# The up blocks of a Strassen feed-forward computed product by product, two halves of the moving side in one matmul

## The chip, the cores and the metric

The kernel runs on one core of one Trainium2 chip. The metric is the device time of that core in microseconds (us), from one launch. [...]

## The reference, cut to what matters

One decoder layer for 512 positions and a model width of 2048, all in float32. The change lies in the last part, a gated convolutional MLP:

```python
h = rmsnorm(x, pre_ffn_g[l])
up = causal_depthwise_conv(h @ w_up[l], conv_w[l], conv_b[l])     # 2048 -> 2 x 5632, 3 taps
gate, val = jnp.split(up, 2, axis=-1)
y = (jax.nn.gelu(gate, approximate=True) * val) @ w_down[l]       # 5632 -> 2048
x = x + rmsnorm(y, post_ffn_g[l])
```

## The kernel before, in words

**Numbers.** Every float32 matrix is split into a rounded part `hi` (fp32r) and the rest `lo`. ACT makes `hi` by a copy with rounding, DVE makes `lo` by a subtraction. A product of two matrices is three passes on PE (`passes`, lines 922 to 924): hi x hi, hi x lo, lo x hi.

**Blocks.** The feed-forward goes through `w_up` in 22 blocks of 256 gate columns and 256 value columns. The first is computed plainly; the other 21 (called s = 1 to 21 here) by Strassen's method in Winograd's form: seven products P1, P2 and Q3 to Q7 of quarter matrices instead of eight. Each product runs over a contraction of 1024, which is 8 steps of 128 rows (`KH`), for two groups of 128 output columns. Between the up blocks stands the down projection of the group before, for s = 2 to 19 again as seven products, each of 12 matmuls of 512 columns (`down_quads`); s = 20 and 21 have a plain one (`down`). A block and the down products behind it are called a half; odd and even halves alternate.

**Order within an up block.** `up` runs `quad` for i = 0 to 7. A quad is one contraction step of all seven products: 7 products x 2 column groups x 3 passes of 256 columns, 42 matmuls, into seven PSUM banks that are all open through the block. So a block needs 336 matmuls of 256 columns.

**What feeds a quad.** SP brings one chunk of weights (128 x 1024, 512 KB) for each quad into the ring `w_raw` of four slots; chunk n + 4 waits until slot n has been read out (`lo_ready`). Three of the seven stationary tiles are quarters of the weights; four are sums, which DVE makes in three instructions (`quad_sum_one`, lines 2755, 2761, 2766: 512, 256 and 256 columns). ACT rounds 768 columns of raw weights (line 1813) and 1024 columns of sums (line 1818); DVE makes both `lo` parts (lines 2777 and 2783). The split weights `w_hl` hold two quads.

**After a block** ACT copies P1's bank (line 1832) and DVE puts the seven banks together into the four quarters of the output (`u_early`, `u_late`, `u_last`; lines 2868 to 2883), in the time of the down products. Those start with quarter weights (`raw_form_hi`, `raw_form_lo`) and go on to sums of quarters (`first_sum`, `second_sum`, `right_sum`, `third_sum`; lines 2833 to 2847, their `lo` parts line 2810). ACT carries each down product out of PSUM (`leave_product`, line 1911), and POOL adds it to a scratch in HBM by a DMA (line 824). In the same queue DVE does the convolution's taps (line 2900), gate x value (line 2921), and once for each pair of halves, within the even block, the sums and `lo` parts of the activations for the down products (lines 2934 to 2967).

**Order on the queues** is written by hand: `quad_round` and the dictionaries of tasks on DVE and ACT say behind which quad each of the other tasks stands. Every engine works its own queue strictly in that order.

**Elsewhere in the kernel** the input projections already run in the other way: `chain_half` (lines 1109 and 1111) takes one product at a time over half a contraction, with hi and lo of the moving side side by side in one matmul of 512 columns (hi x hi and hi x lo), and lo x hi in one of 256.

Of the kernel before, what the change touches and what calls it, by code (L numbers as in the profile page):

```python
# [24 lines left out]
F32 = mybir.dt.float32  # L25
# [63 lines left out]
RAW_PLACE = {P1: 0, Q3: 4, P2: 6}  # L89
COLUMN = {P1: 0, Q3: 1, P2: 2, Q5: 3, Q7: 4, Q6: 5, Q4: 6}  # L90
SPLIT_W = 7 * HB
RAW_W = 3 * HB
DOWN_BANKS = (7, P1, Q6, P2, Q7, Q4, Q3, Q5)
# [3 lines left out]
FORM_SLOT = (0, 1, 3, 2, 0, 3, 2)  # L97
# [3 lines left out]
AFTER_SUBS = (Q3, Q5, P1, Q6, P2, Q7, Q4)  # L101
# [13 lines left out]
def sums_before(g, e):  # L115
    w = half_index(g, e)
    return KH + PER_HALF * min(w, QUAD_HALVES) + KH * max(w - QUAD_HALVES, 0)
# [40 lines left out]
def build_layer(nc, xT, x, w, rope, decay, mix_g, ws_t, ln_g, ln_b, b_s, post_mix_g, pre_ffn_g, conv,  # L158
                post_ffn_g, rs_dram, x2_dram, y8_dram, gates_dram, sgu_dram, ret_dram, out):
    with ExitStack() as ctx:  # L160
# [13 lines left out]
        b_hi = at("b_hi", 64, [NG, S], F32R)  # L174
        b_lo = at("b_lo", 80, [NG, S], F32R)
# [20 lines left out]
        r3_hi = at("r3_hi", 160, [KH, HB], F32R)  # L196
        r3_lo = at("r3_lo", 168, [KH, HB], F32R)
        r4_lo_b = at("r4_lo_b", 188, [KH // 2, HB], F32R)
        r4_hi = at("r4_hi", 192, [KH, HB], F32R)
        r4_lo_a = at("r4_lo_a", 200, [KH // 2, HB], F32R)  # L200
# [116 lines left out]
        sums_even = flat[:, 0:4 * HB].rearrange("p (a s) -> p a s", a=2)  # L317
        sums_odd = wsum_odd
# [36 lines left out]
        def sums(i):  # L355
            return sums_odd if i % 2 else sums_even

        def product_form(k):
            a = FORM_SLOT[k] * 2 * CK * NB
            return w_flat[:, a:a + CK * NB], w_flat[:, a + CK * NB:a + 2 * CK * NB]  # L360

        def form_room(k):
            a = FORM_SLOT[k] * 2 * CK * NB + CK * NB
            return w_gap[:, :, :].rearrange("p a s -> p (a s)")[:, a:a + CK * NB]
# [34 lines left out]
        def operand(p, k):  # L399
# [9 lines left out]
            return hi.rearrange("p a s -> p (a s)"), lo.rearrange("p a s -> p (a s)")  # L409

# [47 lines left out]
        rs_row = ps[P1]  # L458

# [152 lines left out]
        out_done = sem("out_done")  # L612

# [304 lines left out]
        def _(pe):  # L918
# [321 lines left out]
            def quad(c, i, order, free={}):  # L1240

                pe.wait_ge(lo_ready, c + (i + 1))
                w_h, w_l = quad_split(i)
                for p in order:
                    if p in free:
                        pe.wait_ge(*free[p])
                    for n in range(2):
                        col = slice(COLUMN[p] * HB + n * P, COLUMN[p] * HB + n * P + P)
# [120 lines left out]
        def _(act):  # L1369
# [604 lines left out]
            def quads(c, n, tasks):  # L1974

                for i in range(2, KH):
                    quad_hi(c, i, c + (i - 1))
                    quad_sum_hi(n + i, i)
                    if i in tasks:
                        tasks[i]()  # L1980
# [1285 lines left out]
```

## Time and profile before

| | us |
|---|---|
| median of 3 runs | 2534.92 |
| lowest, highest | 2531.77, 2536.95 |
| the profiled execution | 2535.78 |
| its span, first to last instruction | 2533.9 |

The page of the profile gives busy time by engine (PE 2516.5 us, DVE 2075.3, ACT 1332.9) and the granted clock of PE. How long work takes is the duration in the rows; how fast an engine gets through a queue is the distance between starts, which is shorter, since an instruction starts before the one ahead of it has quite ended. An idle time in a row is followed by what ended it.

### The profile page before, as it was taken

The page shows a single profiled execution, that of the slowest core. Times are in us where ns is not written, and L with a number is a line of the kernel's source. Part 1 is how long each engine was busy: PE and PEld are TensorE (multiplying, and loading weights), DVE is VectorE, ACT ScalarE, POOL GpSimd, SP SyncE. Part 2 cuts the span into 40 slices and gives each one's busy share as a digit, 9 for nine tenths or more (in the row PEclk, how much of TensorE's full clock was granted, in tenths as well). Part 3 has the DMA queues.
Part 4 walks back from the last instruction along what each step waited for, and adds up shares of the span by engine and source line. Part 5 has one row for each costly group of instructions (what it writes and reads, how often), then busy time and mean ns, then how long its engine had stood idle before and what let it go on. Part 6 is the DMA issues. An engine that isn't in the chain of part 4 may idle for free. (4 is left out here: it accounts for less than half of the span.)

```text
span 2533.9 us, 40321 instructions
## 1 busy us (share of the span) xinstructions
PE 2516.5 (99%) x15762; PEld 2272.9 (90%) x15762; DVE 2075.3 (82%) x2517; ACT 1332.9 (53%) x1690; POOL 184.4 (7%) x271
## 2 busy tenths in 40 slices
PE   9999999999999999999999999999999999999998
PEld 8888888888888888888999999999999999999997
DVE  8898888888888545436898989898999989898987
ACT  8554545555555322335545656555555555555544
POOL 0100000000000000000000011100000000001122
PEclk9999999999999999999999999999999999999999
DMA  6434343333243723434234466666666666666878
GB/s 258 146 114 144 125 141 115 106 120 120 97 161 133 283 99 133 148 126 172 81 104 167 159 174 174 177 173 174 173 171 167 167 161 163 167 166 160 256 234 289
DMA packets 106765, 405.42 MB, mean 160 GB/s; under 512 B 12432, under 2 KB 12448, under 8 KB 100960
## 3 DMA queue, kind: packets, MB, share of 16 engines
q1 hardware_dynamic: 72576, 263.76, 30.7%
q0 software_dynamic: 33728, 138.71, 21.1%
q8 instruction: 124, 2.03, 0.3%
q10 hardware_dynamic: 288, 0.52, 0.1%
q14 instruction: 49, 0.40, 0.0%
HBM read 303.33 MB, written 95.42 MB: 157 GB/s over the span
## 5 line engine op out<-in xcount | busy, mean ns | idle before, releaser
L922 PE MATMUL ps<-h_both,w_hl 128*128 128x256 f32 (+1 forms) x1360 | 416.2, 306 | 1.0 <-DVE w_hl L2783 0.8
L923 PE MATMUL ps<-h_both,w_hl 128*128 128x256 f32 (+1 forms) x1360 | 415.4, 305 | 0.0
L924 PE MATMUL ps<-h_both,w_hl 128*128 128x256 f32 (+1 forms) x1360 | 415.4, 305 | 0.0
L1813 ACT ACTIVATE w_hl<-w_raw 128x768 fp32r<-128x768 f32 x168 | 142.3, 847 | 342.1 <-PE ps L924 342.1
L1109 PE MATMUL ps<-rm_both,w_hl 128*128 128x512 f32 x896 | 318.2, 399 | 1.3 <-DVE w_hl L2262 0.8
L922 PEld LDWEIGHTS ps<-h_both,w_hl 128*128 128x128 f32 x1360 | 259.8, 191 | 13.6 <-DVE w_hl L2783 1.5
L923 PEld LDWEIGHTS ps<-h_both,w_hl 128*128 128x128 f32 x1360 | 259.9, 191 | 11.2
L924 PEld LDWEIGHTS ps<-h_both,w_hl 128*128 128x128 f32 x1360 | 259.8, 191 | 11.2
L922 PE MATMUL ps<-w_hl,h_both 128*128 128x512 f32 (+1 forms) x684 | 261.6, 382 | 1.1 <-issue 0.6
L923 PE MATMUL ps<-w_hl,h_both 128*128 128x512 f32 (+1 forms) x684 | 261.2, 382 | 0.0
L924 PE MATMUL ps<-w_hl,h_both 128*128 128x512 f32 (+1 forms) x684 | 261.0, 382 | 0.0
L1111 PE MATMUL ps<-rm_both,w_hl 128*128 128x256 f32 x896 | 250.5, 280 | 0.0
L1109 PE MATMUL ps<-h_both,w_hl 128*128 128x512 f32 x672 | 237.8, 397 | 1.6 <-DVE shared L2323 1.3
L2125 DVE TENSOR_TENSOR w_hl<-w_raw,w_hl 128x1024 fp32r<-128x1024 f32 x75 | 91.4, 1223 | 161.7 <-ACT w_hl L1386 161.0
L2777 DVE TENSOR_TENSOR w_hl<-w_raw,w_hl 128x768 fp32r<-128x768 f32 x168 | 160.4, 955 | 61.0 <-ACT w_hl L1813 60.9
L1109 PEld LDWEIGHTS ps<-rm_both,w_hl 128*128 128x128 f32 x896 | 168.2, 188 | 42.4 <-DVE w_hl L2262 1.4
L1504 ACT ACTIVATE w_hl<-w_t 128x1024 fp32r<-128x1024 f32 x108 | 114.4, 1060 | 158.3 <-PE ps L1111 85.3
L922 PE MATMUL ps<-r_hi,w_hl 128*128 128x256 f32 x672 | 190.2, 283 | 0.6 <-ACT work L1911 0.6
L924 PE MATMUL ps<-r_hi,w_hl 128*128 128x256 f32 x672 | 190.2, 283 | 0.0
L923 PE MATMUL ps<-b_lo,w_hl 128*128 128x256 f32 x672 | 190.2, 283 | 0.0
L922 PE MATMUL ps<-b_hi,w_hl 128*128 128x256 f32 x672 | 190.2, 283 | 0.0
L924 PE MATMUL ps<-b_hi,w_hl 128*128 128x256 f32 x672 | 190.2, 283 | 0.0
(387 smaller groups left out, 6463.8 us busy)
## 6 DMA issues: line engine op xcount, KB each, us to landing
w_raw<-in_w SPq DMA_DIRECT2D x487, 512.0 KB, 3.8
y_scratch<-work POOLq DMA_DIRECT2D x78, 512.0 KB, 9.5
y_scratch<-forms_f POOLq DMA_DIRECT2D x29, 512.0 KB, 13.0
y_scratch<-big POOLq DMA_DIRECT2D x27, 512.0 KB, 7.6
gate_scratch<-mixing POOLq DMA_DIRECT2D x8, 1024.0 KB, 6.1
mixing<-in_x POOLq DMA_DIRECT2D x4, 1024.0 KB, 6.7
mixing<-mixing POOLq DMA_DIRECT2D x16, 256.0 KB, 3.7
merged<-gate_scratch POOLq DMA_DIRECT2D x4, 1024.0 KB, 12.6
```

What stands on the lines that cost most here:

```text
L922: pe.matmul(bank, s_hi, m_hi_, start=first, stop=False, skip_group_check=skip)
L923: pe.matmul(bank, s_hi, m_lo_, start=False, stop=False, skip_group_check=skip)
L924: return pe.matmul(bank, s_lo, m_hi_, start=False, stop=last, skip_group_check=skip)
L1109: pe.matmul(bank.rearrange("p (a s) -> p a s", a=2), s_h, m_both, start=p in (P1, Q5) and k == 0, stop=False, skip_group_check=True)
L1111: mm = pe.matmul(bank[:, 0:HB], s_l, m_h, start=False, stop=k == KH - 1, skip_group_check=True)
L1504: act.activation(w_hl[:, form_slot(n, f), 0, :], src, ACT.Copy, scale=-1.0 if p in (Q6, Q7) else 1.0)\
L1813: act.activation(hi[:, 0:RAW_W], w_raw[:, i % RING, HB:], ACT.Copy).then_inc(hi_ready, 1)
L2125: TTm(w_hl[:, j, 1, :], w_raw[:, j, :], w_hl[:, j, 0, :].bitcast(F32), ALU.subtract).then_inc(lo_ready, 1)
L2777: TTm(lo[:, 0:RAW_W], w_raw[:, i % RING, HB:], hi[:, 0:RAW_W].bitcast(F32), ALU.subtract)
```

## The change

All 21 up blocks now run as the input projections do. A block is 14 half-forms f = 0 to 13: product f // 2 of the chain P1, Q5, Q6, Q3, Q7, P2, Q4, half f % 2 of its contraction. A half-form is 4 steps x 2 column groups x (one matmul of 512 + one of 256), and takes one of four slots of `w_hl`, each 1024 columns wide:

```diff
-            def quad(c, i, order, free={}):
...
-                for p in order:
...
-                    for n in range(2):
-                        col = slice(COLUMN[p] * HB + n * P, COLUMN[p] * HB + n * P + P)
-                        mm = passes(ps[p][:, n * HB:n * HB + HB], (w_h[:, col], w_l[:, col]), operand(p, i),
-                                    i == 0 and n == 0, i == KH - 1, True)
...
+            def up_half_form(s, f):
+
+                p, a, slot = CHAIN[f // 2], f % 2, slots_of(s)[f % RING]
...
+                pe.wait_ge(*up_lo_made(s, f))
...
+                if p == Q6 and a == 0:
+                    pe.wait_ge(up_seeded, s)
+                if p == Q3 and a == 0:
+                    pe.wait_ge(u_step, 6 * s - 5)
+                if p == Q7 and a == 0:
+                    pe.wait_ge(u_step, 6 * s - 4)
+                if p == Q4 and a == 0:
+                    pe.wait_ge(u_step, 6 * s - 2)
+                for kk in range(4):
+                    k = 4 * a + kk
+                    o_h, o_l = operand(p, k)
+                    for m in range(2):
+                        bank, c = pair[:, m * NB:m * NB + NB], slice(kk * HB + m * P, kk * HB + m * P + P)
+                        pe.matmul(bank.rearrange("p (a s) -> p a s", a=2), w_hl[:, slot, 0, c], operand_both(p, k),
+                                  start=p in (P1, Q5) and k == 0, stop=False, skip_group_check=True)
+                        mm = pe.matmul(bank[:, 0:HB], w_hl[:, slot, 1, c], o_h, start=False, stop=k == KH - 1,
+                                       skip_group_check=True)
```

The products add up in three pairs of banks. `u_step` counts DVE's steps of a block in the order q5, x2, c12, c22, c11, c21: so f6 waits for q5 (`up_q5`), f8 for x2 (`up_x2`), f12 for c22. ACT copies one half of a pair out for each (`up_half_q5` and its like) and once seeds a pair from another (`up_seed`). The sums of weights are made for half a product at a time, in `up_t`, with t-one from chunks a and 2 + a, t-two adding chunk 4 + a, t-three and t-four:

```diff
+            def up_t_one(s, a):
...
+                TTm(up_t[a], up_raw(s, a), up_raw(s, 2 + a), ALU.add).then_inc(lo_ready, 1)
...
+            def ups(s, tasks, start=2):
+
+                for f in range(start, FORMS):
+                    if f == 7:
+                        up_q5(s)
+                    if f == 9:
+                        up_x2(s)
+                    if f == 12:
+                        up_c12_first(s)
+                    if f == 13:
+                        up_c22_first(s)
+                        up_c12(s)
+                        up_c22(s)
+                    up_lo_of(s, f)
...
+                    if f in (3, 4):
+                        up_t_two(s, f - 3)
...
+                    if f in tasks:
+                        tasks[f]()
...
             def quad_half(g, e, tasks):
...
+                third_sum(s)
+                up_lo_of(s + 1, 0)
+                sum_form_lo(s, 6)
+                up_t_one(s + 1, 0)
+                up_lo_of(s + 1, 1)
+                up_t_one(s + 1, 1)
                 if e:
                     gate_taps(g, e)
```

`up_lo_of` stands at line 2904 or 2906 of the changed kernel, t-one at 2920, t-two 2925, t-three 2931, t-four 2938, the steps c12 and c22 at 3006 to 3022, taps at 3045, down `lo` parts at 2942. On ACT the matching end of a half reads: down form 6, hi of f0, leave 4, hi of f1, leave 5, leave 6, then for odd halves `gate_linear`, and then hi of f2:

```diff
                 leave_product(g, e, 3)
-                sum_form_hi(g, e, 6)
-                quad_hi(c, PER_HALF, c + PER_HALF - 1)
-                quad_sum_hi(n + PER_HALF, PER_HALF)
+                sum_form_hi(s, 6)
+                up_hi(s + 1, 0)
                 leave_product(g, e, 4)
+                up_hi(s + 1, 1)
                 leave_product(g, e, 5)
...
                 leave_product(g, e, 6)
```

Line 824's stores, the number and size of chunks and the rule by which SP waits stay as they are; the order of the quarters in the chunks changes.

**DVE at the end of an odd half's down products.** Before, from `third_sum` (L2847): three small sums of quad 0, the `lo` of the last down form (L2810), the parts of quads 0 and 1; the taps follow behind four more rows of quads 1 and 2.

```order
L2847 TENSOR_TENSOR w_gap<-big,w_raw 128x1024
L2755 TENSOR_TENSOR big<-w_raw 128x512
L2761 TENSOR_TENSOR big<-big,w_raw 128x256
L2766 TENSOR_TENSOR big<-big,w_raw 128x256
L2810 TENSOR_TENSOR w_hl<-w_gap,w_hl 128x1024
L2777 TENSOR_TENSOR w_hl<-w_raw,w_hl 128x768
L2755 TENSOR_TENSOR w_gap<-w_raw 128x512
L2783 TENSOR_TENSOR w_hl<-big,w_hl 128x1024
L2761 TENSOR_TENSOR w_gap<-w_gap,w_raw 128x256
L2766 TENSOR_TENSOR w_gap<-w_gap,w_raw 128x256
L2755 TENSOR_TENSOR big<-w_raw 128x512
```

Now, from `third_sum` (L2982) at the same place:

```order
L2982 TENSOR_TENSOR w_gap<-big,w_raw 128x1024
L2906 TENSOR_TENSOR w_hl<-w_raw,w_hl 128x1024
L2942 TENSOR_TENSOR w_hl<-w_gap,w_hl 128x1024
L2920 TENSOR_TENSOR big<-w_raw 128x1024
L2906 TENSOR_TENSOR w_hl<-w_raw,w_hl 128x1024
L2920 TENSOR_TENSOR ps<-w_raw 128x1024
L3045 SCALAR_TENSOR_TENSOR big<-big,shared 128x511 x2
L3045 SCALAR_TENSOR_TENSOR big<-big,shared 128x510 x2
L2906 TENSOR_TENSOR w_hl<-big,w_hl 128x1024
```

The `lo` of f0 now stands ahead of the last down form's, and the sum of chunks 1 and 3 (L2920 into ps) and four taps stand ahead of the `lo` of f2.

**DVE at the end of an even up block.** Before, the last activation parts, then the down forms, with the recombination (L2868 to L2873) among them:

```order
L2959 TENSOR_TENSOR h_both<-big,h_both 128x2x256
L2965 TENSOR_TENSOR f_lo<-work,f_hi 128x1024
L2967 TENSOR_TENSOR s_lo<-big,s_hi 128x512
L2833 TENSOR_TENSOR big<-w_raw 128x1024
L2810 TENSOR_TENSOR w_hl<-w_raw,w_hl 128x1024 x2
L2868 TENSOR_TENSOR big<-ps,big 128x2x256
L2869 TENSOR_TENSOR big<-ps,big 128x2x256
```

Now, from t-four (L2938):

```order
L2938 TENSOR_TENSOR big<-big,w_raw 128x1024
L2938 TENSOR_TENSOR ps<-ps,w_raw 128x1024
L3104 TENSOR_TENSOR h_both<-big,h_both 128x2x256
L3006 TENSOR_TENSOR big<-ps,big 128x2x256
L2906 TENSOR_TENSOR w_hl<-big,w_hl 128x1024
L3110 TENSOR_TENSOR f_lo<-work,f_hi 128x1024
L3112 TENSOR_TENSOR s_lo<-big,s_hi 128x512
L3012 TENSOR_TENSOR big<-big,ps 128x2x256
L3017 TENSOR_TENSOR big<-ps,big 128x2x256
L3022 TENSOR_TENSOR big<-big,ps 128x2x256
L2906 TENSOR_TENSOR w_hl<-ps,w_hl 128x1024
```

L3022 is the step c22 for which PE's f12 waits; it now stands inside the block, behind the activation parts.

## Rows read from the trace of the kernel before

**Rows 1.** The page: the span, and busy time of each engine (share, instructions).
```profile
span 2533.9 us, 40321 instructions
PE 2516.5 (99%) x15762; PEld 2272.9 (90%) x15762; DVE 2075.3 (82%) x2517; ACT 1332.9 (53%) x1690; POOL 184.4 (7%) x271
```
**Rows 2.** Waits of PE over the whole span: us in total, times, longest.
```profile
PE ps L1109 <- DVE shared L2323: 1.3, 2, 0.8
...
PE ps L922 <- DVE w_hl L2783: 0.8, 2, 0.6
```
**Rows 3.** Busy time by stretch: input projections, then up blocks (us, engines, clock, DMA).
```profile
400.00:600.00 200.00, 199.30 (x1194) 175.46 (x1193) 167.20 (x195) 111.74 (x183) 8.28 (x14) 1.00 0.35 113
...
2000.00:2200.00 200.00, 200.00 (x1443) 190.04 (x1443) 182.45 (x242) 116.62 (x136) 18.76 (x22) 1.00 0.67 177
```
**Rows 4.** PE in order of time, an up block: start us, duration us, line.
```profile
1655.08 0.28 PE L923 MATMUL ps<-h_both,w_hl 128*128 128x256 f32 x1
...
1659.88 0.28 PE L924 MATMUL ps<-h_both,w_hl 128*128 128x256 f32 x1
```
**Rows 5.** PE in order of time, the last down products, and the next block's first matmul.
```profile
1696.12 0.39 PE L924 MATMUL ps<-w_hl,f_lo 128*128 128x512 f32 x1
...
1702.24 0.39 PE L924 MATMUL ps<-w_hl,h_both 128*128 128x512 f32 x1
1702.47 0.28 PE L922 MATMUL ps<-r_hi,w_hl 128*128 128x256 f32 x1
```
**Rows 6.** PE in order of time, an input projection with 512 and 256 columns alternating.
```profile
299.65 0.39 PE L1109 MATMUL ps<-h_both,w_hl 128*128 128x512 f32 x1
299.88 0.27 PE L1111 MATMUL ps<-h_both,w_hl 128*128 128x256 f32 x1
...
303.81 0.39 PE L1109 MATMUL ps<-h_both,w_hl 128*128 128x512 f32 x1
```
**Rows 7.** DVE in order of time, an up block and the recombination behind it.
```profile
1601.17 1.22 DVE L2783 TENSOR_TENSOR w_hl<-big,w_hl 128x1024 fp32r<-128x1024 f32 x1
1602.31 0.42 DVE L2766 TENSOR_TENSOR w_gap<-w_gap,w_raw 128x256 f32<-128x256 f32 x1
1602.65 1.40 DVE L2900 SCALAR_TENSOR_TENSOR big<-big,shared 128x510 f32<-128x510 f32 x2
1603.97 0.68 DVE L2755 TENSOR_TENSOR big<-w_raw 128x512 f32<-128x512 f32 x1
...
1622.91 0.68 DVE L2868 TENSOR_TENSOR big<-ps,big 128x512 f32<-128x512 f32 x1
1623.51 0.68 DVE L2869 TENSOR_TENSOR big<-ps,big 128x512 f32<-128x512 f32 x1
```
**Rows 8.** ACT in order of time: activation parts, P1's copy, a down form's hi.
```profile
1665.20 0.61 ACT L1944 ACTIVATE h_both<-work 128x512 fp32r<-128x512 f32 x1
1665.72 1.04 ACT L1945 ACTIVATE h_both<-big 128x1024 fp32r<-128x1024 f32 x1
...
1679.59 0.58 ACT L1832 ACTIVATE big<-ps 128x512 f32<-128x512 f32 x1
...
1690.59 1.06 ACT L1928 ACTIVATE w_hl<-w_gap 128x1024 fp32r<-128x1024 f32 x1 [3.16 <-DVE w_gap L2842]
```
**Rows 9.** DVE in order of time, the down products of one half into the next block.
```profile
1697.47 1.22 DVE L2810 TENSOR_TENSOR w_hl<-w_gap,w_hl 128x1024 fp32r<-128x1024 f32 x1
...
1703.82 0.69 DVE L2755 TENSOR_TENSOR big<-w_raw 128x512 f32<-128x512 f32 x1 [1.74 <-DMA w_raw<-in_w]
...
1707.62 0.69 DVE L2755 TENSOR_TENSOR w_gap<-w_raw 128x512 f32<-128x512 f32 x1 [0.43 <-DMA w_raw<-in_w]
```
**Rows 10.** Transfers of chunks 1 and 2, issued at 1693.1 and 1693.7: us from issue to landing.
```profile
DMA to landing us min/median/max: 4.4/7.3/10.1
```
**Rows 11.** The same of chunk 3, issued at 1698.8.
```profile
DMA to landing us min/median/max: 8.8/8.8/8.8
```
**Rows 12.** The page's DMA issues: KB each, median us from issue to landing.
```profile
w_raw<-in_w SPq DMA_DIRECT2D x487, 512.0 KB, 3.8
```

More of the change, by code:

```diff
@@ L1255, in up @@
-            def up(c, free, order=ORDER):
-                for i in range(KH):
-                    quad(c, i, *((order, free) if i == 0 else (ORDER,)))
+            def up_half_form(s, f):
+                p, a, slot = CHAIN[f // 2], f % 2, slots_of(s)[f % RING]
+                x, y, z = chain_banks(s)
+                pair = {Q5: z, Q3: z, P2: y}[p] if p in (Q5, Q3, P2) else x
+                pe.wait_ge(*up_lo_made(s, f))
+                if p == P1 and a == 0:
+                    if s == 1:
+                        pe.matmul(y[:, 0:NB], h_hi[:, 0, 0:P], h_hi[:, 0, :], start=True, stop=True)
+                        pe.wait_ge(plain_left, 2)
+                    elif s == 2:
+                        pe.wait_ge(u_step, 3)
+                    else:
+                        pe.wait_ge(*pair_left(s, "x"))
+                if p == Q5 and a == 0:
+                    if s == 1:
+                        pe.wait_ge(plain_left, 3)
+                    elif s == 2:
+                        pe.wait_ge(u_step, 6)
+                    else:
+                        pe.wait_ge(*pair_left(s, "z"))
+                if p == Q6 and a == 0:
[15 more added lines that the diff above has]
+                                       skip_group_check=True)
+                mm.then_inc(up_used(s, f)[0], 1)
@@ L1974, in quads @@
[L1974 to L1980, printed above, removed]
-            quads(C_SUB1, 0, {2: lambda: gate_linear(0, 0), 3: lambda: val_linear(0, 0), 4: lambda: gelus(0)})
-            quad_hi(C_LOOP, 0, C_LOOP - 1)
-            quad_sum_hi(KH, 0)
-            leave_p1(1)
-            quad_hi(C_LOOP, 1, C_LOOP)
-            quad_sum_hi(KH + 1, 1)
@@ L1989, in quad_half @@
[L1989 to L2001 removed]
+            up_hi(1, 0)
@@ new lines, in _, with ups @@
+            up_hi(1, 1)
+            act.wait_ge(r_lo, 4 * TT)
+            for t in range(4):
+                bank = done(A, FFN_USE, t, C_SUB1)
+                dst = (u_gate, u_val)[t // 2][:, t % 2, :]
+                act.activation(dst, bank, ACT.Copy).then_inc(plain_left, 1)
+            def ups(s, tasks):
+                for f in range(2, FORMS):
+                    if f == 5:
+                        up_seed(s)
+                    if f == 7:
+                        up_half_q5(s)
+                    if f == 9:
+                        up_half_x2(s)
+                    up_hi(s, f)
+                    if f in tasks:
+                        tasks[f]()
@@ L3215, in sub @@
     def sub(n):
-        quads(np.concatenate([a[:, n * HB:n * HB + HB] for a in (gate, val)], axis=1))
+        chain(np.concatenate([a[:, n * HB:n * HB + HB] for a in (gate, val)], axis=1))
     add(np.concatenate([gate[:, :HB], val[:, :HB]], axis=1))
```

682 lines of the change are left out of this document (371 added, 311 removed).

## The prediction

> **What bounds the kernel now.** The page comes first: PE is busy 2516.5 of 2533.9 us, DVE 2075.3, ACT 1332.9 [rows 1]. The list of PE's waits is short, and its longest entries for DVE come to 1.3 and 0.8 us over the whole run [rows 2]. So PE's own stream is the bound, and what shortens it shortens the kernel, as long as the others keep up. How much room they have is read by stretch: in the input projections, which already run in the new form, DVE is busy 167.20 of 200 us; in the up blocks it is 182.45 of 200 [rows 3]. That 9% is all the slack there is where the change lands, and PE's clock shows 1.00 in both.
>
> **What the stream gains.** In an up block the matmuls of 256 columns start 40 intervals apart in 4.80 us, 0.120 us each [rows 4]. In the down products 27 intervals of 512 columns take 6.12 us, 0.2267 us each [rows 5]. Where 512 and 256 alternate, twelve pairs take 4.16 us, 0.3467 us a pair [rows 6]: the sum of the two. A triple of 256 takes 0.360 us, so a pair saves 0.0133 us. That is one instruction's overhead; the columns are the same 768. A block has 7 x 8 x 2 = 112 triples: 112 x 0.0133 = 1.49 us, and 21 blocks give 31.4 us. A half (block and down products) is now 336 x 0.120 + 84 x 0.2267 = 40.32 + 19.04 = 59.36 us, and without any wait would be 38.83 + 19.04 = 57.87. A half-form takes 8 x 0.3467 = 2.77 us, a down product 12 x 0.2267 = 2.72.
>
> The Trainium skill (TensorE: Matmul & The Clock Gate, on back-to-back matmuls) puts the overhead of a warm matmul at about 2.5 ns above its columns. By it the saving would be 21 x 112 x 2.5 ns = 5.9 us, an estimate. The trace disagrees: 512 columns at 2.4 GHz are 213.3 ns and the starts are 226.7 apart [rows 5].
>
> **What DVE has to do.** Through a queue, 1024 columns cost DVE 1.14 us from start to start (1601.17 to 1602.31), a pair of taps 1.32, and 512 columns 0.60 (1622.91 to 1623.51) [rows 7]; whoever waits for one waits for its end, 1.22 or 0.68 after its start. For ACT the ends count: 1.04 to 1.06 us for 1024 columns, 0.61 for 512, 0.58 for a copy out of PSUM [rows 8]. A block's weight work on DVE is now 14 `lo` parts and 8 sums of 1024 and 8 steps of 512: 22 x 1.14 + 8 x 0.60 = 29.9 us, about what it was. So the amount is no term. The place is: six of the eight recombining steps move from the time of the down products into the block, where PE's f6, f8 and f12 wait for them, and the queue is in order.
>
> **The term that decides: chunk 3.** In the even halves DVE does the following between the sum of chunks 1 and 3 and the step c22: four taps 2.64, eleven `lo` (f2 to f12) 12.54, six sums 6.84, four more taps 2.64, gate x value 1.14, six steps 3.60, the activations' parts and sums 6.5. Together 35.9 us. PE goes from the start of f0 to the start of f12 in 12 x 2.77 = 33.3 us. So that sum must be done 2.6 us before f0 starts, or PE waits at f12 for all of the difference. It cannot be. Chunk 3 goes into the slot that the `lo` of the last down form sets free, and that `lo` ends 2.7 us before f0 at the earliest that matters, since PE's last down product (2.72 us) waits for it. (In the trace of before it ended at 1698.7 [rows 9], and chunk 3 was issued at 1698.8 [rows 11].) It may even end later: from the end of the fourth down product it takes `third_sum` 1.22, ACT's hi of the down form 1.05, ACT's hi of f0 0.95 more, then DVE's `lo` of f0 1.14 and the `lo` itself 1.22, with the hand-overs 5.9 us in all; PE has two products, 5.4 us, so it waits 0.45 us there in every half. Before, three small sums (1.3 us) stood there in place of the hi and `lo` of f0.
>
> How long chunk 3 takes to land I bound from both sides: chunk 1, alone in the queue, took 4.4 us, chunks 2 and 3, with stores around them, 10.1 and 8.8 [rows 10, 11]. In the trace of before they came 1.35 and 5.1 us after the block's start (1702.47 [rows 5] against 1703.82 and 1707.62 [rows 9]), and nobody on PE minded, since quad 2 is due only after 10 us. Now f2 is due 5.5 us after f0, and its `lo` stands behind the sum that needs chunk 3. I take 4.4 us behind the issue, the nearer row: DVE's queue in the down products is lighter by the recombination, so chunks 1 and 2 are asked for 11.8 us ahead of f0 (before: 1702.47 - 1693.1 = 9.4) and have landed when chunk 3 is asked for. Issued at f0 - 2.7, it lands at f0 + 1.7.
>
> **Even half, step by step**, in us after f0's start. Chunk 3 lands 1.7; sum 2.9; four taps to 5.5; `lo` of f2 ends 6.7, and f2 was due 5.55: PE waits **1.2**. Then `lo` f3, t-two, taps, `lo` f4, t-two, taps, `lo` f5 to 15.1, on time (f5 is due 15.1). Gate x value ends 16.2; ACT then rounds the activation's parts (0.52 + 0.95) and only then copies Q5's half, 18.3; q5 ends 19.0, f6 was due 17.8: **1.2**. `lo` f7, two sums t-three, two activation parts, `lo` f8, two activation sums, then x2, which ends 27.7; f8 was due 24.6: **3.2**. After that the hi of f11 waits for its slot, which PE leaves only at 30.5, and ACT's own activation parts; `lo` f11 starts 33.3; two t-four, an activation part, c12, `lo` f12, two activation parts, c22 first, c12, c22: 42.7. f12 was due 38.8: **3.9**. With 0.45 at the last down product the even half has 9.9 us of waits: 57.87 + 9.9 = 67.8 us.
>
> **Odd half.** No activation parts (6.5 us less), and the four early taps stand elsewhere. The same walk: f5 0.6 (t-two needs chunk 5, which is asked for only after chunk 3's sum), f6 1.9 (ACT has `gate_linear` ahead of Q5's copy), f8 1.0 (a tap pair ahead of x2), f12 0.6, the last down product 0.45: 4.5 us, 62.4 us.
>
> The same walk through the queues of before, with the same durations and the same rule for chunks, gives 59.4 us for a half, no wait of PE, and a wait of DVE for chunk 2 in each half, which is what the trace shows [rows 2, 9].
>
> **The sum.** Even blocks s = 4 to 18, eight: +79. Odd 5 to 19, eight: +36. s = 2 and 3, whose stores are lighter: +12. s = 1, 20, 21, with little beside them: +4. Less 31.4: +100 us. The profiled execution took 2535.8, so 2636; the median lies 0.9 below it: **2635 us**.
>
> **Ends of the range.** With every chunk landing 3.4 us after its issue (the page's median over all chunks is 3.8 [rows 12]) the walk still has 67.6 and 60.4 for the halves: about 2618. With 5 us behind each other, between the rows' 4.4 and 8.8, it has 69.6 and 65.5: about 2677. If my order of hand-overs is too strict everywhere except in the 35.9 us of the even half, what is left is 33.3 - 35.9, the chunk's landing at f0 + 0.7 and the sum: 5 us in nine even halves and 0.45 in eighteen, 53 - 31 = +22: 2557.
>
> **Rivals.** (1) Faster: the chain runs as it does in the input projections, where the longest entry among PE's waits is 1.3 us for all blocks together [rows 2]. Then the kernel gives 2535 - 31 = 2504. It decides at one point: the sum with chunk 3 must end 2.6 us ahead of f0. For it speaks that the total of DVE fits (92% of the time); against it, that there no down product stands between two blocks, and that DVE is at 84% [rows 3]. (2) DVE late only by the 35.9 us: 2557 to 2580. (3) The clock falls in the pauses of 3 to 4 us. The trace has only 1.00, and no PE wait above 2 us, so the price is bounded from the step: one half-form after each of the two long waits at 1.2 instead of 2.4 GHz costs 2 x 2.77 us in nine even halves, 50 us: 2685. The Trainium skill (TensorE: Matmul & The Clock Gate, on the clock gate) says that the clock falls to 1.2 GHz after an idle stretch; no row here shows one.
>
> **How the numbers follow.** Walk as forecast, 2590 to 2680: 0.80. Rival 1: 0.07. Rival 2: 0.06. Rival 3: 0.04. Something slight, within the bound: 0.03. The range 2570 to 2682 leaves out rival 1, the bottom of rival 2 and the clock's case. A measurement of this kernel can tell about 0.2% from no change, 5 us; faster by more 0.07, within 0.03, slower 0.90.
>
> **What would show it.** In the changed kernel's page, DVE and ACT lines as releasers of the 512-column matmul of the up blocks with some 110 to 130 us of idle in total, most of it under x2 and c22 in even halves; halves alternating near 68 and 62 us; a DVE wait for a transfer before the sum into ps; pairs 0.347 us apart in between. I am wrong if the list of PE's waits stays within a few us, or if the waits sit at `lo` parts alone, or if chunk 3 lands before f0.

## The result, and the profile after

The changed kernel takes 2698.57 us (median of 4 runs, 2698.15 to 2698.97); the kernel before took 2534.84 us in the same comparison (2531.77 to 2536.95). The ratio is 1.065, with a 95% interval of 1.0637 to 1.0664. The change costs 163.7 us. The prediction said 2635 with a range of 2570 to 2682: slower was right, the size was not, and the time lies outside the range.

The page of the changed kernel: span, busy time of each engine with its share and instructions, then the chain of work that ended last, by engine. In all rows PE is TensorE's matmuls, PEld its weight loads, DVE is VectorE, ACT ScalarE, POOL GpSimd, and SP is SyncE, whose queue issues the weight transfers.

```profile
span 2697.1 us, 35558 instructions
PE 2551.6 (95%) x13411; PEld 2173.1 (81%) x13411; DVE 2056.2 (76%) x2181; ACT 1386.8 (51%) x1732; POOL 184.9 (7%) x271
...
PE 58%; DVE 20%; DMA 9%; issue 6%; ACT 5%; SPq 0%; DVEq 0%; ACTq 0%
```

Against [rows 1], TensorE fell from 99% to 95% busy. Its busy time rose by 35 us all the same, though its stream is shorter: matmuls at a slower clock, which count as busy, are a part of it, and we come to them. Its waits (us in total, times, longest) stand against [rows 2]:

```profile
PE ps L1357 <- DVE w_hl L2906: 64.0, 18, 5.5
PE ps L1357 <- DVE big L3000: 29.7, 19, 2.8
PE ps L1357 <- DVE big L3022: 15.0, 10, 2.3
PE ps L1357 <- DVE big L2995: 12.1, 12, 4.2
PE ps L1005 <- DVE w_hl L2942: 6.6, 18, 0.4
```

L1357 is the new matmul of 512 columns. L3000 is x2, L3022 c22, L2995 q5, L2942 the `lo` of a down form: the four that the prediction names, with 63.4 us together. The largest entry is another one: 64.0 us behind a `lo` part, L2906. In order of time, one even half and the first wait of the odd half behind it (start us, duration, the wait in brackets; f0 starts at 1824.08 and 1896.48):

```profile
1834.88 0.79 PE L1357 MATMUL ps<-b_both,w_hl 128*128 128x512 f32 x1 [4.99 <-DVE w_hl L2906]
1848.82 0.47 PE L1357 MATMUL ps<-r_all,w_hl 128*128 128x512 f32 x1 [0.61 <-DVE big L2995]
1857.37 0.47 PE L1357 MATMUL ps<-r_both,w_hl 128*128 128x512 f32 x1 [2.76 <-DVE big L3000]
1871.05 0.47 PE L1357 MATMUL ps<-h_both,w_hl 128*128 128x512 f32 x1 [2.34 <-DVE big L3022]
...
1904.67 0.50 PE L1357 MATMUL ps<-b_both,w_hl 128*128 128x512 f32 x1 [2.38 <-DVE w_hl L2906]
...
```

The first row is f2, and it waits 4.99 us; the walk had given it 1.2. What VectorE did there, in order of time, against [rows 9]:

```profile
1819.96 1.22 DVE L2942 TENSOR_TENSOR w_hl<-w_gap,w_hl 128x1024 fp32r<-128x1024 f32 x1
1822.03 1.22 DVE L2920 TENSOR_TENSOR big<-w_raw 128x1024 f32<-128x1024 f32 x1 [0.86 <-DMA w_raw<-in_w]
1823.17 1.22 DVE L2906 TENSOR_TENSOR w_hl<-w_raw,w_hl 128x1024 fp32r<-128x1024 f32 x1
1829.82 1.23 DVE L2920 TENSOR_TENSOR ps<-w_raw 128x1024 f32<-128x1024 f32 x1 [5.42 <-DMA w_raw<-in_w]
1830.96 2.73 DVE L3045 SCALAR_TENSOR_TENSOR big<-big,shared 128x511 f32<-128x511 f32 x4
1833.60 1.22 DVE L2906 TENSOR_TENSOR w_hl<-big,w_hl 128x1024 fp32r<-128x1024 f32 x1
```

The `lo` of the last down form ends at 1821.2 and frees chunk 3's slot. Chunk 3 is asked for at 1821.3, which is f0 - 2.8, as the prediction had it. VectorE then stands still for 5.42 us. The transfer's own row (us from issue to landing), the answer to [rows 11]:

```profile
DMA to landing us min/median/max: 8.4/8.4/8.4
```

So chunk 3 lands at f0 + 5.7 and not at f0 + 1.7. Behind it come the sum, four taps and the `lo` of f2, and TensorE waits. The chain that ended last says the same, piece by piece (start us, us, what):

```profile
1821.34 8.36 DMA w_raw<-in_w
1829.82 1.23 DVE ps L2920
1831.05 2.65 DVE big L3045 x4
```

The clock did what the third rival said. Stretches of that half: us, busy time of PE, PEld, DVE, ACT and POOL, PE's granted clock, DMA share, GB/s.

```profile
1824.08:1829.90 5.82, 5.80 (x33) 4.78 (x31) 0.40 (x2) 3.38 (x4) 0.85 (x1) 1.00 1.05 261
1832.00:1834.80 2.80, 0.00 (x0) 0.00 (x0) 2.80 (x4) 1.02 (x2) 0.00 (x0) 0.50 1.07 234
1834.88:1837.00 2.12, 2.12 (x7) 1.83 (x8) 0.76 (x1) 1.33 (x2) 0.00 (x0) 0.50 0.65 245
1837.00:1840.00 3.00, 3.00 (x14) 2.57 (x14) 3.00 (x5) 1.37 (x2) 0.00 (x0) 0.70 0.00 0
1840.00:1848.00 8.00, 8.00 (x47) 6.85 (x45) 6.92 (x8) 5.72 (x9) 0.00 (x0) 1.00 0.00 1
```

In the last 2.8 us of the pause the granted clock is 0.50, that is 1.2 of 2.4 GHz, and f2 begins at that level. The last slow matmul of 512 columns starts at 1838.24 and takes 0.63 us, the next one 0.39; from 1840 on the row has 1.00. f2 to f5 take 13.3 us (from 1834.88 to 1848.82, less the 0.61 of f6's wait) in place of 4 x 2.77 = 11.1. Behind each of the eight waits at f2 of 4.8 us and more the work starts at 0.50. Behind the shorter ones of the odd halves it differs from half to half: it stays at 1.00 behind the 2.38 us at 1904.67, and is 0.50 in the 2.8 us behind waits of 2.45 and 2.44 us at 1630.6 and 1767.6. The Trainium skill (TensorE: Matmul & The Clock Gate, on the clock gate) says that the clock falls to 1.2 GHz after an idle stretch; the trace agrees for the wait of 5 us.

The last number in each row is worth a look too. While chunk 3 is on its way the DMA engines are busy all the time (1.05, 1.07: measured shares of 16 engines run slightly over 1); ten microseconds later they move nothing (0.00).

### The profile page after: what moved, and what is told of

It is laid out like the page before. It is cut to its first block, busy times and chain, and to the rows that moved or that the text cites. A ratio compares the mean times of both kernels' runs of the same rounds, so it can differ in the third digit from the quotient of the medians.

```text
span 2697.1 us, 35558 instructions
## 1 busy us (share of the span) xinstructions
PE 2551.6 (95%) x13411; PEld 2173.1 (81%) x13411; DVE 2056.2 (76%) x2181; ACT 1386.8 (51%) x1732; POOL 184.9 (7%) x271
## 3 DMA queue, kind: packets, MB, share of 16 engines
q0 software_dynamic: 33728, 138.71, 20.0%
## 4 chain that ended last, share of the span: by engine, by line
PE 58%; DVE 20%; DMA 9%; issue 6%; ACT 5%; SPq 0%; DVEq 0%; ACTq 0%
PE ps L1192 13%; PE ps L1005 8%; DMA w_raw<-in_w 8%; PE ps L1007 8%; PE ps L1006 8%; PE ps L1357 7%; PE ps L1194 7%; PE ps L1359 4%; DVE big L3045 3%; DVE w_hl L2904 2%; ACT w_hl L1925 2%; DVE w_hl L2906 2%; DVE w_raw L2931 1%; DVE w_hl L2942 1%; DVE w_hl L2407 1%
## 5 line engine op out<-in xcount | busy, mean ns | idle before, releaser
L1357 PE MATMUL ps<-h_both,w_hl 128*128 128x512 f32 x1008 | 358.3, 398 | 15.8 <-DVE big L3022 15.0
L1357 PE MATMUL ps<-b_both,w_hl 128*128 128x512 f32 x672 | 264.4, 431 | 66.1 <-DVE w_hl L2906 63.2
L1359 PE MATMUL ps<-h_both,w_hl 128*128 128x256 f32 x1008 | 282.9, 281 | 0.0
L1357 PEld LDWEIGHTS ps<-h_both,w_hl 128*128 128x128 f32 x1008 | 190.0, 188 | 64.2 <-issue 17.9
L1192 PE MATMUL ps<-h_both,w_hl 128*128 128x512 f32 x672 | 237.7, 397 | 1.3 <-DVE shared L2466 1.3
L1925 ACT ACTIVATE w_hl<-w_raw 128x1024 fp32r<-128x1024 f32 x168 | 176.5, 1051 | 97.0 <-DVE w_raw L2931 67.9
L1357 PEld LDWEIGHTS ps<-b_both,w_hl 128*128 128x128 f32 x672 | 139.1, 207 | 106.9 <-DVE w_hl L2906 68.6
L2268 DVE TENSOR_TENSOR w_hl<-w_raw,w_hl 128x1024 fp32r<-128x1024 f32 x75 | 91.4, 1223 | 162.5 <-ACT w_hl L1484 161.8
L1192 PEld LDWEIGHTS ps<-rm_both,w_hl 128*128 128x128 f32 x896 | 168.2, 188 | 42.4 <-issue 1.6
L1359 PE MATMUL ps<-b_both,w_hl 128*128 128x256 f32 x672 | 199.6, 297 | 0.0
L2906 DVE TENSOR_TENSOR w_hl<-w_raw,w_hl 128x1024 fp32r<-128x1024 f32 x126 | 153.8, 1221 | 58.4 <-ACT w_hl L1925 58.4
L1359 PEld LDWEIGHTS ps<-h_both,w_hl 128*128 128x128 f32 x1008 | 191.0, 189 | 0.8
L1194 PE MATMUL ps<-h_both,w_hl 128*128 128x256 f32 x672 | 187.8, 279 | 0.0
L1484 ACT ACTIVATE w_hl<-w_raw 128x1024 fp32r<-128x1024 f32 x71 | 74.8, 1057 | 204.1 <-PE ps L1007 202.0
L1194 PEld LDWEIGHTS ps<-rm_both,w_hl 128*128 128x128 f32 x896 | 169.1, 189 | 0.0
L1602 ACT ACTIVATE w_hl<-w_raw 128x1024 fp32r<-128x1024 f32 x108 | 114.0, 1056 | 95.4 <-PE ps L1194 92.2
```

Source lines behind the costliest of these rows:

```text
L1192: pe.matmul(bank.rearrange("p (a s) -> p a s", a=2), s_h, m_both, start=p in (P1, Q5) and k == 0, stop=False, skip_group_check=True)
L1194: mm = pe.matmul(bank[:, 0:HB], s_l, m_h, start=False, stop=k == KH - 1, skip_group_check=True)
L1357: pe.matmul(bank.rearrange("p (a s) -> p a s", a=2), w_hl[:, slot, 0, c], operand_both(p, k), start=p in (P1, Q5) and k == 0, stop=False, ...
L1359: mm = pe.matmul(bank[:, 0:HB], w_hl[:, slot, 1, c], o_h, start=False, stop=k == KH - 1, skip_group_check=True)
L1602: act.activation(w_hl[:, form_slot(n, f), 0, :], src, ACT.Copy, scale=-1.0 if p in (Q6, Q7) else 1.0)\
L1925: act.activation(w_hl[:, slots_of(s)[f % RING], 0, :], src, ACT.Copy, scale=-1.0 if p in (Q6, Q7) else 1.0)\
```

## The experiments

All of them start from the changed kernel unless said otherwise, and each was compared with the kernel before on the same chip, which took 2535.1 to 2535.7 us. To compare the kernels inside, the start of one operation is used, the first sum of the down forms, which occurs once in each half. In the changed kernel:

```profile
1734.86 1.21 DVE L2966 TENSOR_TENSOR big<-w_raw 128x1024 f32<-128x1024 f32 x1
...
1798.88 1.21 DVE L2966 TENSOR_TENSOR big<-w_raw 128x1024 f32<-128x1024 f32 x1
...
1871.96 1.21 DVE L2966 TENSOR_TENSOR big<-w_raw 128x1024 f32<-128x1024 f32 x1
```

One step is 64.0 us and the next 73.1. From the first to the eighteenth of these starts are 8.5 pairs of halves, and the table gives the mean pair. The two steps of a pair depend on where in its queue VectorE has this sum (the kernel before, with plain stores, shows 57.8 and 60.9, while TensorE has two equal halves), so the table compares only the pair.

| kernel | median us | pair of halves, us |
|---|---|---|
| before, plain stores | 2533.23 | 118.5 |
| changed kernel | 2698.57 | 136.1 |
| early release | 2637.12 | 129.1 |
| filled wait | 2702.76 | 136.3 |
| plain stores | 2634.84 | 128.8 |
| three passes | 2708.36 | 137.2 |
| early release, even halves reordered | 2594.35 | 124.2 |
| early release, short taps | 2602.28 | 126.0 |
| early release, plain stores | 2621.97 | 127.3 |
| both halves reordered | 2592.59 | 123.9 |
| even halves reordered, three passes | 2601.30 | 124.7 |
| both reordered, plain stores | 2562.13 | 120.7 |
| the same, three passes | 2564.26 | 120.7 |

### Chunk 3 is asked for earlier

Chunks 1, 2 and 3 of the next block may come when the last reader of their slots is done. These readers are `right_sum` and `third_sum`; the changed kernel waits for the `lo` parts behind them.

```
-                TTm(form_room(w, 4), down_raw(s, B22), down_raw(s, B12), ALU.subtract).then_inc(sum_ready, 3)
+                TTm(form_room(w, 4), down_raw(s, B22), down_raw(s, B12), ALU.subtract).then_inc(lo_ready, 2)
...
-                TTm(form_room(w, 6), down_sum, down_raw(s, B21), ALU.subtract).then_inc(sum_ready, 3)
+                TTm(form_room(w, 6), down_sum, down_raw(s, B21), ALU.subtract).then_inc(lo_ready, 1)
```

> The weight buffers of chunks 1 and 2 of the next block are handed back when the subtraction of the right sum has read them, and that of chunk 3 when the third sum has, no longer with the low parts of forms 4 and 6. Theory (chunk 3's landing sets f2): the transfer of chunk 3 starts some 3 us earlier, t-one of chunks 1 and 3 waits about 3 us less than the 5.3 us of the changed kernel, the wait at f2 falls from 5.0 us to about 2 in the even half, the clock stays at 1.00 there, and the pair of halves takes about 131 us in place of 137: 2640 to 2660 us. Rival (VectorE has too much to do anyway): the wait only moves from f2 to f6, f8 and f12, and the time is above 2685 us.

Measured: 2637.12 us (2632.97 to 2638.13), ratio 1.0403 (1.0386 to 1.0421), 61 us less than the changed kernel, and the clock over the run 0.995 in place of 0.981. TensorE's waits:

```profile
PE ps L1357 <- DVE big L3004: 30.3, 20, 2.8
PE ps L1357 <- DVE big L2999: 22.0, 18, 4.1
PE ps L1357 <- DVE big L3026: 16.2, 10, 2.4
PE ps L1357 <- ACT ps L1938: 9.7, 10, 1.1
...
PE ps L1357 <- DVE w_hl L2909: 4.2, 9, 0.9
```

The 64 us behind the `lo` of f2 (here L2909) are 4.2. The landing is as slow as it was (8.3 us); it only starts at 1793.7, 7.2 us ahead of f0 (1800.91), and so ends at f0 + 1.1. Some 18 us moved to q5 (L2999, 12.1 to 22.0) and to P1's copy (L1938, 1.5 to 9.7); the rest of the wait is gone, and with it 27 us of busy time (2551.6 to 2524.9), in which the slow matmuls behind the wait have their part. The first theory holds; the time lies 3 us below its range.

### The wait filled with matmuls

```
+                if f == 2 and s > 2:
+                    pe.wait_ge(*pair_left(s, "z"))
+                    for _ in range(20 if s % 2 == 0 else 8):
+                        pe.matmul(z[:, 0:NB].rearrange("p (a s) -> p a s", a=2), b_both[:, 0, 0, 0:P],
+                                  operand_both(Q5, 0), start=True, stop=True)
```

> While TensorE waits at f2 it now runs matmuls of 512 columns into the pair that Q5 is about to start: 20 in an even half (4.5 us at 0.2267), 8 in an odd one (1.8 us). They add nothing to the result. Theory (the pause costs clock): the granted clock stays at 1.00 through f2 to f5, which take 11.1 us in place of 13.05, and of that 2 us in each even half a part comes back at the end: 2660 to 2680 us. Rival (VectorE sets the pace, the slow matmuls ran in time that would have been waited): clock 1.00 too, but the waits at f6 and f8 grow by the same 2 us: 2693 to 2703 us. If the clock falls anyway, the pause is not its cause.

Measured: 2702.76 us (2697.83 to 2703.12), the pair 136.3. Two windows of an even half, the filled wait and the stretch behind it:

```profile
1832.43:1837.56 5.13, 4.73 (x23) 3.58 (x21) 5.00 (x6) 1.10 (x2) 0.00 (x0) 1.00 1.05 251
1837.56:1842.00 4.44, 4.44 (x25) 3.92 (x26) 3.08 (x4) 2.02 (x3) 0.00 (x0) 1.00 0.28 109
```

The clock stays at 1.00 here (over the whole run 0.994, against 0.981), so it was the pause that lowered it, and nothing is won: the waits at q5 and at f4, for P1's copy, grow from 12.1 and 1.5 us to 20.7 and 8.7 over the run. The rival holds. The slow matmuls ran in time that TensorE would have spent waiting for VectorE. The clock is a result of the wait and cost nothing here that could be measured.

### Plain stores, and the control

```
-                        pool.dma_start(y_range(e, p), staged_pair(stage(n)), accum_op=ALU.add).then_inc(landed, 16)
+                        pool.dma_start(y_range(e, p), staged_pair(stage(n))).then_inc(landed, 16)
```

> The stores of the down products write plainly in place of accumulating in memory, which leaves the accumulation over the groups out. Theory (the accumulating stores hold chunk 3 back): its landing falls from 8.4 us to about 5, the wait at f2 by about 3 us in each half, and the kernel takes 2640 to 2665 us. Rival (chunks 1, 2 and 3, asked for within 5 us, share the engines among themselves): the landing stays above 7.5 us and the time above 2690 us.

Measured: 2634.84 us (2629.21 to 2637.08), ratio 1.039 (1.0373 to 1.0407). Chunk 3 is asked for at 1801.6, which is f0 - 2.8 as in the changed kernel, and this is its landing:

```profile
DMA to landing us min/median/max: 3.7/3.7/3.7
```

That is one half. Over the sixteen halves s = 4 to 19 chunk 3 lands 3.5 to 6.6 us after its issue, 4.8 on average, against 8.2 to 9.1 and 8.5 in the changed kernel; the issue is at f0 - 2.7 or f0 - 2.8 in all of them. Chunk 4 is asked for 1.2 us behind it here, nearer than the 2.0 us of the changed kernel, so its neighbour among the chunks is not what made it slow. The time is 5 us below the theory's range.

The page's DMA queue of the stores (packets, MB, share of 16 engines) in this kernel:

```profile
q0 software_dynamic: 33728, 138.71, 14.4%
```

The changed kernel's page has, with the same bytes:

```profile
q0 software_dynamic: 33728, 138.71, 20.0%
```

So the accumulating stores take 1.4 times the engine time of plain ones for the same megabytes, and beside them the chunk lands after 8.5 us on average instead of 4.8. The control is the same edit in the kernel before:

> The control for the plain stores: the kernel before with stores that do not accumulate (the accumulation is left out). It has no wait for a chunk in these blocks, so the time should stay at 2535 us within 5. If it falls by more, a part of what plain stores gave the changed kernel had nothing to do with chunk 3.

Measured: 2533.23 us (2532.20 to 2534.78), ratio 0.9993 (0.9983 to 1.0002): no change. In this kernel the cost of the stores is paid only where somebody is waiting for a chunk.

### Both together

> Early release and plain stores together (the accumulation is left out). Each alone took the wait at f2 nearly away. If they remove the same wait, together they give little more than either: 2620 to 2637 us. If they act on different things (the one on when chunk 3 is asked for, the other on something that runs through the whole half), the gains add up: below 2600 us.

Measured: 2621.97 us (2619.36 to 2625.29). 15 us under early release alone, where the 61 and 64 us of each do not add up. In the main they remove the same wait, by its start and by its length; the number lies at the low end of what was expected.

### Three passes again

```
-                        pe.matmul(bank.rearrange("p (a s) -> p a s", a=2), w_hl[:, slot, 0, c], operand_both(p, k),
-                                  start=p in (P1, Q5) and k == 0, stop=False, skip_group_check=True)
+                        pe.matmul(bank[:, 0:HB], w_hl[:, slot, 0, c], o_h,
+                                  start=p in (P1, Q5) and k == 0, stop=False, skip_group_check=True)
+                        pe.matmul(bank[:, HB:], w_hl[:, slot, 0, c], o_l, start=False, stop=False, skip_group_check=True)
```

> The one matmul of 512 columns over hi and lo is taken apart again into two of 256; the order of the products and everything else stays. By the rows a block streams 1.49 us longer, 31.4 us in all. Theory (the waits hang on VectorE and the chunks, TensorE has slack beside them): most of it goes into shorter waits, some 0.2 us a half stay: 2700 to 2708 us. Rival (the chain goes through TensorE): the whole 31 us come on top, 2725 to 2732 us.

Measured: 2708.36 us (2707.83 to 2712.37), ratio 1.0682 (1.0664 to 1.07): 9.8 us above the changed kernel, just past the upper end of what the theory gave. The starts are the 0.120 us of [rows 4] again:

```profile
1850.59 0.28 PE L1357 MATMUL ps<-b_both,w_hl 128*128 128x256 f32 x1
1850.71 0.28 PE L1359 MATMUL ps<-b_both,w_hl 128*128 128x256 f32 x1
1850.83 0.28 PE L1360 MATMUL ps<-b_both,w_hl 128*128 128x256 f32 x1
```

In the changed kernel 21 pairs of one matmul of 512 and one of 256 columns, without a wait, lie between these starts:

```profile
1840.28 0.40 PE L1357 MATMUL ps<-b_both,w_hl 128*128 128x512 f32 x1
...
1847.70 0.40 PE L1357 MATMUL ps<-b_both,w_hl 128*128 128x512 f32 x1
```

That is 0.353 us a pair and not the 0.3467 of [rows 6]. The last up block (s = 21) has no wait in either kernel and takes 39.56 us merged, 40.31 us with three passes and in the kernel before: merging saves 0.75 us a block, 16 us in 21 blocks, half of the 31.4 that the expectation and the prediction count. 9.8 of the 16 reach the end. The kernel with three passes is the change without its merging: the new order alone costs 173 us (2708.4 - 2535.3). In the even half shown, the chain that ended last goes from chunk 3's landing to f12 through VectorE and ScalarE and not once through TensorE, so a shorter stream has nowhere to act there. In the odd half behind it the chain is back on TensorE from f8 on.

### VectorE's row in the even half

On top of the early release, the same operations in another order: x2 ahead of `lo` f8, the steps of c12 and c22 ahead of `lo` f12, the products behind q5, the first gate taps into the wait for chunk 3. ScalarE's row is reordered to match. From VectorE's row:

```
+                up_t_three(s, 0)
+                up_t_three(s, 1)
+                up_x2(s)
+                up_lo_of(s, 8)
+                first_forms_lo(g - 1)
...
+                up_t_four(s, 1)
+                up_c12_first(s)
+                up_c22_first(s)
+                up_c12(s)
+                up_c22(s)
+                up_lo_of(s, 12)
```

> On top of the early release, the even halves' work on VectorE and ScalarE stands in another order: the sums x2 and c12, c22 ahead of the low parts of f8 and f12, the products and first forms behind q5 and the low part of f6, the gate's first taps into the wait for chunk 3, its linear part ahead of the last product's leaving. No operation is added or left out. Theory (in the even half TensorE waits for the place of an operation in VectorE's row as much as for its amount): the waits at f4, f6 and f8 nearly go, f12 keeps some 3 us because VectorE has 56 us of work in a half of 58; an even half falls from 68.6 to 62 to 64 us, and the kernel takes 2570 to 2595 us. Rival (the amount alone decides, the waits only move): within 10 us of 2637.

Measured: 2594.35 us (2593.29 to 2599.36), ratio 1.024 (1.0222 to 1.0257). The order of the two rows was worth 43 us; the time is at the upper end of what was expected. The waits at f4, f6 and f8 of the even halves are gone, f12 keeps 1.6 us in most of them, and f5 has one of 0.4 to 1.1 us in some. The other side is the amount, tested by making the taps short:

```
-                    STT(buf[:, t, n:S], src[:, t, 0:S - n], col(t, k), buf[:, t, n:S], ALU.mult, ALU.add)\
+                    STT(buf[:, t, n:n + 1], src[:, t, 0:1], col(t, k), buf[:, t, n:n + 1], ALU.mult, ALU.add)\
```

> On top of the early release, each of the eight tap operations of a half of the feed-forward part works on one column instead of 510 or 511, so the convolution's taps are left out but for one column; every wait and signal stays. That takes some 4.9 us of VectorE's work from each half. Theory (VectorE is late in the even half, but in the odd half only the landings are): the even half falls by 3 to 5 us, the odd one by under 1 us, 2590 to 2612 us. Rival (not the amount of VectorE's work, but chains of single results): less than 10 us of gain in all.

Measured: 2602.28 us (2598.50 to 2603.20). The total is as expected, its places are not: both alternating distances fall by about the same (68.6 to 66.8 and 60.9 to 59.6). VectorE's busy time falls by 86 us (2055.5 to 1969.3), 3.9 for each of 22 blocks and not the 4.9 of the expectation, and some 8 us less work in a pair shorten it by 3.1. In the odd halves nearly every wait of TensorE is gone; in the even ones those at f6, f8 and f12 stay as they were (1.0, 2.7 and 0.6 to 2.4 us). Removing this work gave less than moving work did.

### The odd half, and what is left

```
+                    if f == 6 and s % 2:
+                        up_q5(s)
+                    if f == 8 and s % 2:
+                        up_x2(s)
```

> On top of the reordered even halves, the odd halves take q5 and x2 ahead of the gate's taps of f6 and f8. In the profile of the reordered kernel TensorE waits 1.16 us for q5 at f6 and 0.76 us for x2 at f8 in an odd half. Theory (these two wait for their place in VectorE's row): both go, some 1.5 to 1.9 us in each of ten odd halves: 2575 to 2582 us. Rival (what is gained at f6 and f8 is waited for at f10 to f12, since the taps then come later): 2590 to 2597 us.

Measured: 2592.59 us (2590.84 to 2595.27), no gain that can be told from none. The waits from f6 on in an odd half, first of the kernel with the even halves reordered, then of this one:

```profile
1869.83 0.47 PE L1357 MATMUL ps<-r_all,w_hl 128*128 128x512 f32 x1 [1.16 <-DVE big L3026]
1876.37 0.47 PE L1357 MATMUL ps<-r_both,w_hl 128*128 128x512 f32 x1 [0.76 <-DVE big L3031]
```

```profile
1874.83 0.47 PE L1357 MATMUL ps<-r_both,w_hl 128*128 128x512 f32 x1 [0.76 <-DVE big L3031]
1887.09 0.47 PE L1357 MATMUL ps<-h_both,w_hl 128*128 128x512 f32 x1 [0.71 <-DVE big L3053]
```

The first fence has q5 (L3026) and x2 (L3031). In the second, the wait for q5 is gone, the one for x2 is as long as it was, and there is a new one for c22 (L3053) at f12: the rival. What else is left shows in the chain that ended last of this kernel, ahead of another block:

```profile
1903.83 1.24 DVE w_gap L3013
1905.21 7.96 DMA w_raw<-in_w
1913.30 1.25 DVE ps L2951
1914.69 8.04 DMA w_raw<-in_w
1922.83 1.23 DVE ps L2956
```

Chunk 3's landing is followed by its sum, which frees a slot for chunk 5, whose landing is followed by the next sum (L2956). Two landings of 8 us stand behind each other between `third_sum` (L3013) and the `lo` of f5 (L2934), and the early release has only shortened what lies around them. That was tested with plain stores on this kernel, and both kernels with three passes beside it:

> The kernel with early release and both orders changed, with plain stores (the accumulation is left out). In the chain that ended last, that kernel's piece from 1842 to 1855 us is a store of 11.6 us whose landing ScalarE waits for before it writes the value tile; in its sister with three passes two landings of chunks, 8.6 and 8.5 us, stand in the same place. Theory (what is left behind TensorE's reordered row hangs on these landings): 2550 to 2575 us. Rival (VectorE's 107 us of work in a pair of halves of 124 set the rest): within 10 us of 2592.

> The kernel with early release and reordered even halves, and the one matmul of 512 columns taken apart into two of 256, as was done to the changed kernel itself, where it cost 9.8 us of the 31.4 that the rows give. TensorE now waits some 60 us in place of 130. Theory (the gain of the longer stream counts as far as the waits around it are gone): 15 to 28 us are lost here, 2609 to 2622 us. Rival (a fixed share of a third counts whatever the waits): 2602 to 2606 us.

> The same with the matmul of 512 columns taken apart into two of 256. Theory (with quick landings the chain runs through TensorE for more of the half, so the stream counts for more than the 7 to 10 us that it did until now): 15 us or more above the kernel with plain stores and one matmul. Rival (VectorE's chain in the even half absorbs it all the same): under 10 us above.

Measured: with plain stores 2562.13 us (2560.67 to 2562.91), 30 us less, as the theory had it. Three passes cost 7.0 us on the kernel with the even halves reordered (2601.30, 2599.88 to 2603.78, against 2594.35) and 2.1 us with plain stores (2564.26, 2562.17 to 2565.73), which these runs cannot tell from none. Both times the theory's number was too high; the first rival missed by 0.7 us, the second was right in its number. Of the 16 us that merging saves on TensorE the three kernels show 9.8, 7.0 and 2.1 at the end. With plain stores TensorE is busy 196.1 of 200 us with one matmul and 198.1 with two, in nearly equal time:

```profile
1800.00:2000.00 200.00, 196.12 (x1030) 165.76 (x1029) 176.87 (x184) 117.89 (x134) 11.18 (x21) 1.00 0.48 165
```

```profile
1800.00:2000.00 200.00, 198.10 (x1409) 186.11 (x1409) 175.51 (x183) 117.79 (x134) 11.18 (x21) 1.00 0.49 163
```

The pair takes 120.7 us in both. The kernel before has 118.8 by its matmuls, 2 x (40.31 + 19.07), up block and down products. With three passes it is TensorE's own stream that fills the pair, not VectorE as the rival said. Its waits over the whole run, the two largest entries:

```profile
PE ps L1005 <- DVE w_hl L2974: 5.6, 18, 0.3
PE ps L1357 <- DVE big L3054: 4.7, 3, 2.1
```

In its sixteen up blocks s = 4 to 19 only one wait is longer than 0.25 us, and a block takes 40.6 or 40.7 us against 40.31. The rest of the difference lies in the down products, 19.7 us against 19.07, of which the `lo` of the last down form (L2974) is 0.3. With one matmul a block takes 40.4 or 40.6 us against 39.56 without waits, and each has a wait of 0.7 or 0.8 us at f12: what the shorter stream saves is waited for there, behind c22 or the `lo` of f12. Of the 26.5 us between this kernel and the one before, 16 lie in three blocks that were not reordered: s = 1 and 2 take 91.2 us together against 80.6, s = 20 takes 45.9 against 40.3.

No version beat the kernel before. The best complete one is 2592.59 us, 2.3% above it.

## Why the prediction was wrong in size

**The stream's gain** was too large twice over. The 0.0133 us a pair comes from the twelve pairs of [rows 6], a quick stretch: over the 1897 pairs of the input projections before without a wait or a low clock the mean is 0.3505 us, and an up block without waits fell from 40.31 to 39.56 us, 0.0067 us for each triple. So TensorE's stream lost 16 us and not 31.4. And taking it off the end was wrong as well: the runs with three passes put what reaches the end at 9.8, 7.0 and 2.1 us. The sum subtracted the gain from waits that it shortens.

**Chunk 3's landing** is the step that failed. The issue at f0 - 2.7 was right (f0 - 2.8), and both bounds were in the text: 4.4 us, chunk 1 alone, and 8.8, chunk 3 itself in [rows 11]. I took 4.4, because chunks 1 and 2 would have landed by then. They had, but for 0.6 us: chunk 2 is asked for at f0 - 11.1 and lands at f0 - 2.2. But the neighbours that matter are the accumulating stores of the down products; with them and the chunks all 16 engines are busy until some 12 us into the block. The row nearest to the case was chunk 3's own, issued at the same place beside the same stores. The size of the step follows: with plain stores the landing is 4.8 us on average, the pair 128.8 us against my 67.8 + 62.4 = 130.2, and the kernel takes 2634.8 us against my 2635. The landing is worth 62 us in 8.5 pairs, about as much as the 64 by which the forecast was too low. That the total meets the forecast so closely with that number put right is luck: the stream's gain was 16 us too large in the same sum, and other terms make up for it. s = 1 and 2 together and s = 20 each took 12 us more than their stream in the changed kernel, where the sum has 16 for s = 1, 2, 3, 20 and 21.

**The even and the odd half.** I had 1.2, 1.2, 3.2 and 3.9 us at f2, f6, f8 and f12 of the even half; measured were 4.99, 0.61, 2.76 and 2.34 in the one shown, and f12 has 0.6 to 2.3 in the eight even halves s = 4 to 18. x2 and the last down product (0.45 against 0.37) are right as waits, though the seven down products grew by 0.67 us, from 19.07 to 19.74, where the sum has the 0.45. f12's wait was put too high in any case: with the early release, where f2's is 0.4 us, f12's is still 0.6 to 2.4. Why, these runs do not show. In the odd half 0.6, 1.9, 1.0 and 0.6 were said for f5, f6, f8 and f12, and 2.38 at f2, 0.56 at f5, 1.15 and 0.67 at f6 and f8 came. The wait of 1 us at f4 for P1's copy, which shows once f2's is gone, I had not seen.

**The upper end of the range** was the walk with landings of 5 us behind each other, 2677. I called 5 a value between the rows' 4.4 and 8.8, and it was no bound. With 8.4 to 8.8 in the place of the upper end the range would probably have held the time; the walk was not worked out for it.

**Rivals.** The first (the chain runs as in the projections, 2504) is out. So is the second, VectorE late only by the 35.9 us at f12. The third, the clock, came true as a fact (0.50 in the wait at f2) and fell as a price: the filled wait gives the clock back and no time.

**The signs to look for.** DVE as releaser of the 512-column matmul with 110 to 130 us: 127 us with the down products' `lo`. Pairs 0.347 us apart: only in places; the mean is 0.351. A wait of VectorE for a transfer ahead of the sum into ps: yes, 5.42 us. Halves near 68 and 62: they were 72.4 and 64.8. "Most of it under x2 and c22": no, half of it under the `lo` of f2, and that was the sign that named the wrong step.

## What to carry to other kernels

- An order that puts a transfer's landing ahead of the first thing TensorE needs turns a landing time nobody noticed into the kernel's price. Take its length from the row of the transfer that will stand in the same place beside the same neighbours, not from the quickest one of its size; where two rows are a factor of two apart, both belong in the range.
- A saving on an engine counts only where the chain runs through it. Here 16 us saved on TensorE were worth 2 to 10; work the walk out with and without the saving before the two are added. And take the saving from a long stretch: the twelve pairs that were read gave twice what a whole block gained.
- Before asking how to make a late engine's work less, ask what stands ahead of the awaited result in its queue: moving operations gave 43 us, taking 3.9 us of work out of every half gave 35.

## What the runs showed of the hardware

- Accumulating stores held the DMA engines for 1.4 times the time of plain stores of the same 138.71 MB (20.0% against 14.4% of 16 engines over the run), and a chunk of 512 KB asked for beside them landed after 8.2 to 9.1 us instead of 3.5 to 6.6.
- Behind the eight waits at f2 of 4.8 to 5.5 us TensorE started at a granted clock of 0.50, and its slow matmuls ended 3.6 to 6.1 us after the start. Behind waits of 2.4 to 3.1 us in the same place the clock was 0.50 in some halves and 1.00 in others. With matmuls in the wait it stayed at 1.00 in the half shown. In this kernel the low clock cost nothing that could be measured.
- One matmul of 512 columns in the place of two of 256, a weight load ahead of each, saved 0.0067 us: 112 such triples took 39.56 us instead of 40.31.
